# A two-block transformer in fp32 on one core: finishing a stage tile by tile, with five split slots of weights

## The reference, cut to what matters

```python
# first block, l = 0, 1: a layer norm after every stage
x = layer_norm(ALPHA * x + hybrid_mixer(x), ...)            # si = 3l      window and dense attention, gating, gates
x = layer_norm(ALPHA * x + memory_cross_attention(x), ...)  # si = 3l + 1
x = layer_norm(ALPHA * x + conv_ffn(x), ...)                # si = 3l + 2
# second block, l = 0, 1: an rms norm ahead of every stage
h = h + mixer_ab(rmsnorm(h)) or conv_module(rmsnorm(h))     # si = 6, 9    sparse attention; 31-tap convolution
h = h + cross_attn(rmsnorm(h), rmsnorm(mem))                # si = 7, 10
h = h + swiglu(rmsnorm(h))                                  # si = 8, 11
```

## Time and profile before

| | |
|---|---|
| median of 3 runs | 3882.6 us (3880.31 to 3888.5) |
| the profiled execution | 3887.2 us, of which the span from first to last instruction 3885.4 us |
| tensor engine (PE) busy | 3585.3 us (92%) |
| vector engine (DVE), scalar engine (ACT), GpSimd (POOL) busy | 1997.5, 1365.9, 389.9 us |
| granted clock of PE, mean | 0.958 |
| moved by DMA | 315.64 MB, 81 GB/s |

### The profile page before, as it was taken

The page is one execution under the profiler, slowest core; times in us unless marked ns, Lnnn a source line. Parts: engine busy times, 40 slices in busy tenths (PEclk is TensorE's granted clock), DMA queues, the critical chain, the costliest instruction groups (busy, mean ns, idle before and its releaser), DMA issues.

```text
span 3885.4 us, 41610 instructions
## 1 busy us (share of the span) xinstructions
PE 3585.3 (92%) x16814; PEld 2908.7 (75%) x16814; DVE 1997.5 (51%) x3122; ACT 1365.9 (35%) x2230; POOL 389.9 (10%) x405
## 2 busy tenths in 40 slices
PE   8999988999998999889998878899999858899999
PEld 7667877888786787778887566778888645778887
DVE  4445355646454454565454874543333895553333
ACT  3333323424234333334333433434233533434232
POOL 1300110000040011000001010200000530210000
PEclk9999999999999999999998899999999879999999
DMA  3101241322221123223221112312222101312222
GB/s 132 60 33 62 96 141 55 103 95 93 84 93 39 54 82 124 88 80 100 98 98 53 34 67 69 109 55 93 96 94 93 60 22 54 106 67 84 100 97 88
DMA packets 88177, 315.64 MB, mean 81 GB/s; under 512 B 10545, under 2 KB 11825, under 8 KB 87473
## 3 DMA queue, kind: packets, MB, share of 16 engines
q1 hardware_dynamic: 87984, 312.98, 23.9%
HBM read 308.75 MB, written 4.19 MB: 81 GB/s over the span
## 4 chain that ended last, share of the span: by engine, by line
PE 71%; DVE 17%; issue 5%; POOL 4%; ACT 3%; DMA 0%; SPq 0%; DVEq 0%; ACTq 0%; POOLq 0%
PE bk L908 61%; PE bk L966 3%; PE bk L1002 3%; DVE ar L1879 3%; DVE wl L1481 2%; PE bk L976 1%; POOL st L1964 1%; DVE wl L1475 1%; POOL st L1962 1%; DVE xl L1488 1%; DVE ar L1799 1%; DVE x L1504 1%; DVE al L1893 1%; POOL x L2021 1%; POOL ar L2058 0%
## 5 line engine op out<-in xcount | busy, mean ns | idle before, releaser
L908 PE MATMUL bk<-xh,wh 128*128 128x512 f32 (+1 forms) x2248 | 857.4, 381 | 52.0 <-DVE xl L1488 28.3
L1475 DVE TENSOR_TENSOR wl<-wr,wh 128x1024 fp32r<-128x1024 f32 x368 | 458.3, 1252 | 811.0 <-ACT wh L1143 810.9
L908 PE MATMUL bk<-xl,wh 128*128 128x512 f32 (+1 forms) x2248 | 851.8, 379 | 0.0
L908 PE MATMUL bk<-xh,wl 128*128 128x512 f32 (+1 forms) x2248 | 851.1, 379 | 0.0
L1143 ACT ACTIVATE wh<-wr 128x1024 fp32r<-128x1024 f32 x368 | 386.3, 1056 | 934.8 <-PE bk L908 892.9
L908 PEld LDWEIGHTS bk<-xh,wh 128*128 128x128 f32 x2248 | 435.0, 194 | 130.5 <-DVE wl L1481 20.2
L908 PEld LDWEIGHTS bk<-xh,wl 128*128 128x128 f32 x2248 | 434.6, 193 | 76.4
L908 PEld LDWEIGHTS bk<-xl,wh 128*128 128x128 f32 x2248 | 435.2, 194 | 74.3
L908 PE MATMUL bk<-wh,ah 128*128 128x512 f32 x1184 | 471.1, 398 | 20.2 <-DVE wl L1481 7.4
L908 PE MATMUL bk<-wl,ah 128*128 128x512 f32 x1184 | 467.3, 395 | 0.0
L908 PE MATMUL bk<-wh,al 128*128 128x512 f32 x1184 | 466.8, 394 | 0.0
(11 more groups left out here) (248 smaller groups left out, 4280.6 us busy)
## 6 DMA issues: line engine op xcount, KB each, us to landing
wr<-in_wpk SPq DMA_DIRECT2D x544, 512.0 KB, 3.3
gb<-in_ln_g SPq DMA_DIRECT2D x6, 512.0 KB, 3.9
gb<-in_ln_b SPq DMA_DIRECT2D x6, 512.0 KB, 5.6
ar<-in_xT SPq DMA_DIRECT2D x4, 512.0 KB, 6.9
ar<-in_memT SPq DMA_DIRECT2D x2, 1024.0 KB, 5.2
x<-in_x SPq DMA_DIRECT2D x4, 512.0 KB, 5.0
park<-x SPq DMA_DIRECT2D x4, 512.0 KB, 6.0
x<-park SPq DMA_DIRECT2D x4, 512.0 KB, 5.0
```

The costliest lines, as they stand in the source:

```text
L908: i = pe.e.matmul(dst, lw, rw, start=g not in opened, stop=end)
L1475: dve.e.tensor_tensor(m.wl[:, s, a], m.wr[:, s, a], m.wh[:, s, a].bitcast(F32), ALU.subtract) \
```

## The change

`wh` and `wl` get five slots (NR), `wr` keeps three (NRAW); the look-ahead is four units. The arena is 220 words smaller, and the area set aside for descriptors of software-made DMAs is cut to 1024 bytes.

At a stage end the last three units (TAIL) are taken tile by tile. Tile 0 and tile 1 are closed (added, bank given back, normed) when they are done; after tile 2's matmuls comes the turn of tile 0; after tile 3's matmuls the rest is a list: turn 1, norm 2, norm 3, turn 2, turn 3 (for si = 2 and 5: turn 1, norm 2, turn 2, norm 3, turn 3). "norm" here holds also the addition to x.

At a stage start with `head=True` the first four units (HEAD), the whole product, are taken tile by tile in a T product and in two halves of the tokens in an F product, and the list is run up to the turn of a tile one unit ahead of the group that needs it. In `cross1` and `cross2` the list is run one entry per unit of the memory's products, and the query product of `cross1` has no head any more.

In attention `oput` comes one step later.

```diff
-NR = 3
-LOOK = 2
-NU = 14700
+NRAW = 3
+NR = 5
+LOOK = 4
+HEAD = 4
+TAIL = 3
+LEAD = 1
+LEADT = 1
+NU = 14480
...
-    def gemm(self, G, evac, pair=False, hooks=None):
+    def gemm(self, G, evac, head=False, tail=None):
...
-        steps, q = [], min(NR, G.nu)
-        if pair:
-            for half in range(2):
+        steps, q = [], min(HEAD, G.nu)
+        if head:
+            groups = [((0,), (0, 1)), ((1,), (2, 3))] if G.orient == "F" else [((t,), (t,)) for t in range(NT)]
+            for n, (part, tiles) in enumerate(groups):
+                if n == 0:
+                    steps.append(("turn", tiles[-1]))
                 for u in range(q):
-                    steps.append((u, outs, half) if G.orient == "F" else (u, outs[2 * half:2 * half + 2], None))
-                if half == 0:
-                    steps.append(None)
+                    if u == max(0, q - (LEAD if G.orient == "F" else LEADT)) and n + 1 < len(groups):
+                        steps.append(("turn", groups[n + 1][1][-1]))
+                    steps.append((u, outs, part[0]) if G.orient == "F" else (u, [part[0]], None))
             steps += [(u, outs, None) for u in range(q, G.nu)]
-        elif hooks is not None:
+        elif tail is not None:
+            q = min(TAIL, G.nu)
             steps += [(u, outs, None) for u in range(G.nu - q)]
-            for half in range(2):
-                for u in range(G.nu - q, G.nu):
-                    steps.append((u, outs[2 * half:2 * half + 2], None))
+            for t in range(NT):
+                steps += [(u, [t], None) for u in range(G.nu - q, G.nu)]
+                steps.append(("tail", t))
...
+    def step_rest(self, n=1):
+        for _ in range(n):
+            if self.rest:
+                kind, si, t = self.rest.pop(0)
+                if kind == "norm":
+                    self.close(si, t)
+                else:
+                    self.turn_x(si, t)
+
+    def turn_upto(self, t):
+        while any(kind == "turn" and tt <= t for kind, _, tt in self.rest):
+            self.step_rest()
+
+    def close(self, si, t):
+        self.add("ev", self.last_res, t)
+        self.give(self.last_res.grp[t])
+        self.norm(si, t)
...
+            def tail(t):
+                if t < 2:
+                    self.close(si, t)
+                elif t == 2:
+                    self.turn_x(si, 0)
+                else:
+                    late = [("norm", si, 2), ("turn", si, 2), ("norm", si, 3)] if si in (2, 5) else \
+                        [("norm", si, 2), ("norm", si, 3), ("turn", si, 2)]
+                    self.rest = [("turn", si, 1)] + late + [("turn", si, 3)]
+            yield from self.gemm(G, None, tail=tail)
...
-        for i in range(n + 4):
+        for i in range(n + 5):
...
-            for f in later:
-                f()
-            later = []
+            if later and later[0][0] < i:
+                later.pop(0)[1]()
...
-                    later.append(lambda t=t, c=q // A.per, no=no: put(t, c, no))
+                    later.append((i + 1, lambda t=t, c=q // A.per, no=no: put(t, c, no)))
...
         G = Gemm(si, "xk", l, 8, (("x_wkv", l, 0, 512),), "mem", "F", 4, width=256)
+        self.step_rest()
+        for _ in self.gemm(G, self.ev(G)):
+            self.step_rest()
+        G = Gemm(si, "xv", l, 8, (("x_wkv", l, 512, 1024),), "mem", "T", 2)
+        for _ in self.gemm(G, self.ev(G)):
+            self.step_rest()
+        G = Gemm(si, "xq", l, 8, (("x_wq", l, 0, 512),), "x", "F", 4)
         drive((self.gemm(G, self.ev(G)), 1))
...
-        self.wr = sb("wr", [128, NR, 1024])
+        self.wr = sb("wr", [128, NRAW, 1024])
...
-        if j + NR < len(sc.units):
+        if j + NRAW < len(sc.units):
             sp.wait_ge(*ev["w_lo", j])
-            weights(j + NR)
+            weights(j + NRAW)
...
-    nc = _bacc.Bacc("TRN2", target_bir_lowering=False, num_devices=1)
+    nc = _bacc.Bacc("TRN2", target_bir_lowering=False, num_devices=1, dynamic_dma_scratch_size=1024)
```

More of the change, by code:

```diff
@@ L182, in __init__ @@
         self.split = self.rel = 0
-        self.pending = []
+        self.rest = []
         self.last_gate, self.last_branch, self.conv_g = {}, {}, None
@@ L238, in gemm @@
                 G.unit[u] = self.use((ks[0], len(ks), G.pieces, gain))
-            self.add("mm", G, u, os_, half, last[u] == j)
-            if ks[-1] == G.nk - 1 and half != 0:
+            self.add("mm", G, u, os_, part, last[u] == j)
+            if ks[-1] == G.nk - 1 and part in (None, 1) and tail is None:
                 for o in os_:
@@ L277, in residual @@
             G = Gemm(si, "res", (hf, first, norm), nk, pieces, op, "T", 4, base=base)
[L279 to L290, removed]
+            if not (norm and si < 11 and hf == 1):
+                yield from self.gemm(G, self.ev(G))
+                continue
+            self.last_res = G
+            def tail(t):
[8 more added lines that the diff above has]
+            yield from self.gemm(G, None, tail=tail)
     def attend(self, A, put):
@@ L356, in proj @@
             G = Gemm(si, "qk", (l, br), 8, (("w_in", l, c0, c0 + 512),), "x", "T", 4)
-            yield from self.gemm(G, self.ev(G), pair=br == "A" and l > 0)
+            yield from self.gemm(G, self.ev(G), head=br == "A" and l > 0)
             G = Gemm(si, "kv", (l, br), 8, (("w_in", l, c0 + 512, c0 + 768),), "x", "T", 4)
@@ L459, in ups @@
                 G = Gemm(si, "up2", (l, m), 8, pieces, "x", "F", 4, gain=("n_ffn", l * 8))
-            return self.gemm(G, self.ev(G), pair=m == 0)
+            return self.gemm(G, self.ev(G), head=m == 0)
         for m in range(0, 12, 2):
@@ L473, in mixer2, with part @@
         scored = {}
-        def part(kind, tag, c0, c1, orient="T", per=None, pair=False, count=None):
+        def part(kind, tag, c0, c1, orient="T", per=None, head=False, count=None):
             G = Gemm(si, kind, tag, 8, (("w_in_ab_2", 0, c0, c1),), "x", orient, 4, gain=gain, per=per)
@@ L482, in evac @@
                     count[0 if len(count) == 1 else tag] += 1
-            return self.gemm(G, evac, pair=pair)
+            return self.gemm(G, evac, head=head)
         def iq_turn(cg, t):
@@ L542, in scoring @@
                 yield
-        drive((part("iq", 0, 2048, 2560, pair=True, count=n_iq), 1))
+        drive((part("iq", 0, 2048, 2560, head=True, count=n_iq), 1))
         drive((chain(lambda: part("ik", 0, 3072, 3152, per=8, count=n_ik),
@@ L611, in evac @@
                         ready.add(m + o - 2)
-                yield from self.gemm(G, evac, pair=m == 0)
+                yield from self.gemm(G, evac, head=m == 0)
             for q, m in enumerate(PEC):
@@ L851, in begin, with mm @@
         return bk[sc.bank[g]]
-    def mm(G, u, outs, half, fin):
+    def mm(G, u, outs, part, fin):
         j = G.unit[u]
@@ L858, in mm @@
         wh, wl = view(m.wh), view(m.wl)
-        c0, c1 = (0, G.width) if half is None else (half * 256, half * 256 + 256)
+        c0, c1 = (0, G.width) if part is None else (part * 256, part * 256 + 256)
         for o in outs:
@@ L906, in mm @@
                 for q, (lw, rw) in enumerate(seq):
-                    end = k == G.nk - 1 and q == 2 and half != 0
+                    end = k == G.nk - 1 and q == 2 and part in (None, 1)
                     i = pe.e.matmul(dst, lw, rw, start=g not in opened, stop=end)
```

50 lines of the change are left out of this document (23 added, 27 removed).

## The result

The changed kernel took **3796.39 us** (median of 4 runs, 3793.98 to 3799.72) beside 3883.13 us for the kernel before on the same chip (4 runs, 3880.31 to 3888.5): ratio 0.9776, 95% interval 0.9759 to 0.9793, 87 us less, against the 72 forecast. The profiled execution took 3799.72 us, its span 3797.9 us.

What follows compares the result with a forecast made beforehand. PE, busy for 3585.3 of 3885.4 us, was taken to bound the kernel. Gains of 55 us (stage ends), 10 (oput) and 7 (look-ahead) summed to 72, forecasting 3810.6 us, range 3760 to 3860.

Steps and rivals of the forecast that it cites:

- Idle at the stage ends: Over the eleven stage ends, PE's idle time was to fall from 93.8 to 50 to 60 us.
- si 0 and 3: Stage ends where 3 us idle and 2 of clock were to be left: gain 9 us each, 18 together.
- si 6 and 9: Stage ends losing the 3.7 us before the key product, but with a later POOL chain: gain 1 us each.
- The clock term: At stage ends, window x (1 - clock) lost to the lower clock, 0.6 of it counted on running matmuls.
- oput, forecast 10: Attention output one step later: of 24.7 us of PE waits, a gain of 10 us.
- Look-ahead of four, forecast 7: Behind the convolution, PE's 5.51 us wait for a weight was to go; with the clock a gain of 7 us.
- elsewhere the depth changes nothing: Away from the convolution the look-ahead was to give no gain, as DVE is not late in the feed-forward stages.
- The rule that speaks against it: POOL instructions slowed beside DVE may stretch each rms chain by 1.1 us, costing 6 to 7 us at si 7, 8, 10.
- deeper gain: Rival: the waits left at si 1, 4 and 5 (24 us) also vanish, about 3760 us; chance 0.16.
- Late norms behind a split that waits for PE: Rival: norms 2 and 3 start only after PE reaches the turn, 98 us over the sum, 3908 us; given little.
- Waits only move: Rival: turns of tiles 2 and 3 wait instead, stage ends give 10 instead of 55 us, 3863 us; chance 0.12.
- The descriptor area: The smaller area for DMA descriptors was counted at nothing: no gain, and no loss unless SP's queue stalls.

Runs made afterwards that it cites:

- depth_alone: The kernel before with five split slots, three raw slots and a look-ahead of four, its order of work unchanged: 3861.73 us, ratio 0.9936 to the kernel before.
- pause_six: The changed kernel with six needless DVE reductions inside tile 0's layer norm at the six layer-norm ends: 3833.29 us, ratio 0.9865 to the kernel before.
- no_weave: The changed kernel, but all four tiles are turned before the next product's first unit: 3867.47 us, ratio 0.9953 to the kernel before.
- tail_one: The changed kernel with one weight unit instead of three finished tile by tile at a stage end: 3867.54 us, ratio 0.9958 to the kernel before.
- cross_spread: The changed kernel with the second block's cross prologue spread out, turns two to four units behind their norms: 3760.83 us, ratio 0.9682 to the kernel before.

## Why the prediction was right

The forecast was 72 us and the result 87, inside the range. Step by step:

**Idle at the stage ends: right.** It wanted 50 to 60 us left of 93.8; its own terms add up to 50, and 45.7 was measured, a little below. End by end (window before minus window after, with forecast): si 0 and 3, 11.6 and 14.9 (9 each); si 1 and 4, 5.7 and 5.3 (3 each); si 2, 8.7 (8); si 5, 6.8 (6); si 6 and 9, 1.3 and -0.8 (1 each); si 7, 8 and 10, 6.4, 5.0 and 6.5 (5 each). Together 71.4, forecast 55. The chain of si 0 came out as told: 1.6 and 0.8 us of waits were foretold, 1.64 and 0.73 are there. At si 6 and 9 the gain did run into the POOL chain: its wait there is 6.04 us behind the norms, where waits of 1.26 and 2.29 stood before. Of the other signs, no turn of x (L955, before L922) waits over 5 us (3.8 at most, at si 5), and between tail and head PE waits 1.7 us at si 7, 8 and 10.

**The clock term was mis-sized.** "Of which I count 0.6 as falling on running matmuls" and 2 us of clock or more left at seven of the ends: of the 55 us, 43 were idle time (93.8 less the 50 left) and 12 clock. Measured were 48.1 and 23.3. Most of the difference stands at si 0 and 3: busy PE fell by 3.6 and 6.8 us there, where the forecast (9, of which 7.4 idle) leaves 1.6 each, and the window of si 3 is at clock 1.00 after the change. Some 0.9 us of each is no clock but the query product's head that is gone, three units at 0.3; other ends pay it back. So 11 of the 16 us by which the ends exceeded their forecast are busy PE, nearly all clock, and 5 are waits a little shorter than in my chains, such as 4.6 instead of 6.5 us at si 1 and 4.

**oput, forecast 10**: 10 to 14 by undoing it. The product with the values did need the same DVE, as said. **Look-ahead of four, forecast 7**: behind the convolution the weight's wait is gone. Windows over the product there, before and after:

```profile
3244.30:3299.90 55.60, 45.15 (x174) 36.12 (x175) 24.62 (x30) 24.80 (x32) 1.68 (x5) 0.85 0.25 95
```

```profile
3171.00:3218.60 47.60, 42.68 (x174) 34.59 (x175) 24.90 (x32) 25.28 (x34) 1.78 (x5) 0.89 0.29 111
```

8.0 us. The convolution ahead of it, foretold as even, took 1.7 us longer (212.3 to 214.0 between the same instructions), so 6.3 are left. But "elsewhere the depth changes nothing" failed: without the look-ahead the changed kernel is 39 us slower, with three units not measurably. Depth alone gave 25 us, reordering and `oput` with three slots 57, and 87 together. So depth and look-ahead are worth 25 to 39 us and not 7: the 55 us of the ends assumed splits made ahead, and the working had no term for that. The sum came out because their worth was in it under another name.

**What ran the other way**: at the start PE waited 7.5 us for the activations, 3.24 before. That is the look-ahead's price, as the experiments show, and the forecast had no term for it: 4.3 us more of waiting, and PE goes on at 22.79 us instead of 19.66.

**The rule that speaks against it** cost nothing where it was feared. All twelve such instructions at si 7, 8 and 10 took 0.19 us. POOL's timeline at si 7, for tiles 0 and 2:

```profile
2551.33 0.19 POOL L1995 TENSOR_SCALAR st<-st 128x1 f32<-128x1 f32 x1 [73.38 <-ACT gb L1197]
...
2568.05 0.19 POOL L1995 TENSOR_SCALAR st<-st 128x1 f32<-128x1 f32 x1 [11.81 <-ACT gb L1197]
```

PE's timeline there, for the earlier trace rows, has one wait between tail and head, at tile 1's copies:

```profile
2565.01 0.36 PE L941 MATMUL bk<-xh,wh 128*128 128x256 f32 x1 [1.67 <-DVE xl L1521]
```

Of the **rivals**, "deeper gain" was nearest; its waits at si 1, 4 and 5 did not vanish (4.6, 4.6 and 9.1 us are left), so it did not hold. Late norms behind a split that waits for PE were not seen: DVE went into norm 2 at 543.84 without a wait. "Waits only move" did hold in depth_alone and for the cross turns. The descriptor area was not tried by itself; it is small in depth_alone and in every kernel derived from the changed one.

## What to carry to other kernels

Where one list sets the order for all engines, the distance in that list between a producer and its reader must cover the producer's whole chain, other engines' work in front of it included: read the chain's length from the timeline (4.2 us alone, 7 to 8 with what stands before it) and put that much PE work between. Deeper buffers bring nothing unless the fill is also listed earlier, and here all of that gain came with one step of it, from two units ahead to three; every further unit makes other work of the same engine wait behind it. The summed wait for a releaser is no forecast of a gain, in either direction: in depth_alone 46 us of such waits went and 25 us of time, in good part because the next stage is bound by the engine that had been late, while at the eleven ends 48 us of idle took another 23 us of busy PE with it.

## What was not expected of the hardware

Idle time taken out of PE gave back clock too, and more than I had counted, but one profile of each kernel can't price it. Per microsecond of idle added or removed against the changed kernel, busy PE moved by 0.21 us in pause_six (6.7 for 31.9), 0.22 in no_weave (12.2 for 54.4), 0.42 in tail_one (20.0 for 47.9) and 0.58 in cross_spread (14.9 for 25.7), with the same number of matmuls in each. Over the eleven ends it was 23.3 for 48.1, 0.48.

Part of that spread is chance. The changed kernel and cross_spread are the same program up to the start of the second block's first cross stage. Windows over that part, the changed kernel first:

```profile
0.00:2371.70 2371.70, 2251.84 (x10812) 1810.52 (x10812) 1289.19 (x2142) 843.30 (x1383) 224.97 (x238) 0.97 0.25 84
```

```profile
0.00:2365.30 2365.30, 2245.21 (x10812) 1805.49 (x10812) 1289.57 (x2142) 843.56 (x1383) 225.02 (x238) 0.97 0.25 84
```

PE's idle time is the same (119.9 and 120.1 us), its busy time 6.6 us apart, nearly all of it in the second block's mixer stage. In that stage all eleven variants of the changed kernel come out 1.4 to 6.5 us below its profiled execution. In the two stages that cross_spread does edit, idle fell by 23.9 us and busy PE by 9.4, a share of 0.39; the other 6.6 us of its 14.9 come from before the edit. Without the second block's mixer stage the shares are 0.46 in pause_six (11.2 for 24.4), 0.33 in no_weave and 0.50 in tail_one. So a good part of the spread from 0.21 to 0.58 is the changed kernel's one profiled execution. What is left, 0.33 to 0.50, is too near the chance seen to tell whether a few long waits and many short ones have different prices. That is open.
